# A third slot for group C's cached keys and values while the units of group B run, asked for three units ahead by two engines

## The reference, cut to what matters

```
A (6 heads): dilated window attention over cache_a_k, cache_a_v        1024 positions
B (6 heads): attention over the 256 keys that an indexer picks          pages of cache_b_k, cache_b_v
C (4 heads): difference of two softmax maps                             pages of cache_c_k, cache_c_v
rows = pool[l, page_table]     # 8 pages of 128 positions per sequence
o = concat(A, B, C) @ w_o
```

## Time and profile before

| what | us |
|---|---|
| median of 3 runs | 1462.43 |
| the 3 runs | 1462.43, 1468.67, 1453.17 |
| the profiled execution, its own time | 1457.15 |
| its span, first to last instruction | 1455.0 |
| TensorE busy in it | 1352.8 (93%) |
| the units of layer one and two, about | 210 to 412, 920 to 1115 |

### The profile page before, as it was taken

The page is one execution under the profiler, slowest core; times in us unless marked ns, Lnnn a source line. Parts: engine busy times, 40 slices in busy tenths (PEclk is TensorE's granted clock), DMA queues, the critical chain, the costliest instruction groups (busy, mean ns, idle before and its releaser), DMA issues.

```text
span 1455.0 us, 23578 instructions
## 1 busy us (share of the span) xinstructions
PE 1352.8 (93%) x8214; PEld 856.8 (59%) x8214; DVE 504.0 (35%) x1315; ACT 286.0 (20%) x711; POOL 62.4 (4%) x271
## 2 busy tenths in 40 slices
PE   6989899988799999999999999998889999999998
PEld 1544346655566666666665543665556567767775
DVE  1102677864254110011012057777534611100112
ACT  0011123333223101100003111433332220100001
POOL 1100000001001000000001000000000100000000
PEclk9999999999899999999999999999999999999999
DMA  7788979999943567887764577899996537686563
GB/s 268 206 288 267 282 234 356 351 283 320 319 142 134 218 218 257 301 317 258 284 224 153 183 233 244 297 373 295 310 320 216 195 130 253 205 284 209 205 235 130
DMA packets 189567, 363.82 MB, mean 250 GB/s; under 512 B 22912, under 2 KB 140360, under 8 KB 187786
## 3 DMA queue, kind: packets, MB, share of 16 engines
q1 hardware_dynamic: 165200, 350.19, 70.6%
q10 hardware_dynamic: 24250, 12.14, 3.3%
HBM read 354.17 MB, written 58.40 MB: 284 GB/s over the span
## 4 chain that ended last, share of the span: by engine, by line
PE 47%; issue 36%; DVE 6%; DMA 3%; SPq 2%; DVEq 2%; ACT 2%; ACTq 1%; POOLq 0%; POOL 0%
PE psf L1004 14%; PE psf L1422 9%; PE psf L1337 4%; PE psf L1192 3%; DMA ring<-in_tiles 3%; PE psf L1026 2%; PE psf L1235 2%; DVE m L1582 2%; DVEq L1585 1%; PE psf L1077 1%; PE psf L1405 1%; SPq L486 1%; PE psf L1281 1%; PE psf L1334 1%; PE psf L1265 1%
## 5 line engine op out<-in xcount | busy, mean ns | idle before, releaser
L1004 PE MATMUL psf<-hT,ring 128*128 128x320 f32 x1440 | 399.2, 435 | 9.6 <-DMA ring<-in_tiles 7.7
L1004 PEld LDWEIGHTS psf<-hT,ring 128*128 128x128 f32 x1440 | 270.5, 190 | 137.9 <-issue 18.2
L1422 PE MATMUL psf<-big,ring 128*128 128x320 f32 x1024 | 280.2, 435 | 4.3 <-DMA ring<-in_tiles 2.2
L1422 PEld LDWEIGHTS psf<-big,ring 128*128 128x128 f32 x1024 | 194.6, 191 | 90.5 <-issue 6.2
L1798 DVE TENSOR_TENSOR big<-sq 128x320 f32<-128x320 f32 x64 | 31.5, 492 | 258.1 <-ACT sq L973 257.8
L1508 DVE TENSOR_SCALAR rstd<-psf,adaT 128x256 f32<-128x256 f32 x32 | 15.4, 482 | 252.9 <-PE psf L1422 237.6
L1582 DVE MAX8 m<-workbuf 64x8 f32<-64x1032 f32 x64 | 78.5, 1226 | 3.0
L931 ACT ACTIVATE sq<-xT 128x320 f32<-128x320 f32 x32 | 15.0, 470 | 324.3 <-DVE xT L1512 324.3
L1584 DVE MATCH_REPLACE8 workbuf<-m,workbuf 64x1032 f32<-64x1032 f32 x64 | 77.4, 1209 | 0.0
L1192 PE MATMUL psf<-big,qs 128*32 128x512 f32 x512 | 70.6, 640 | 6.9 <-issue 5.6
L1026 PE MATMUL psf<-ring,cz 128*32 128x512 f32 x384 | 63.6, 673 | 14.4 <-DVE cz L1456 8.4
(11 more groups left out here) (182 smaller groups left out, 1215.9 us busy)
## 6 DMA issues: line engine op xcount, KB each, us to landing
ring<-in_tiles SPq DMA_DIRECT2D x284, 512.0 KB, 4.4
big<-in_cache_a SPq DMA_DIRECT2D x64, 768.0 KB, 7.1
out_cache_a<-in_cache_a SPq DMA_DIRECT2D x64, 768.0 KB, 5.9
big<-in_pool_bk SPq DMA_DIRECT2D x128, 192.0 KB, 3.7
big<-in_pool_bv SPq DMA_DIRECT2D x128, 192.0 KB, 4.6
big<-in_pool_cv SPq DMA_DIRECT2D x256, 64.0 KB, 4.2
big<-in_pool_ck SPq DMA_DIRECT2D x128, 64.0 KB, 4.1
big<-in_pool_ck ACTq DMA_DIRECT2D x128, 64.0 KB, 4.5
```

What stands on the lines that cost most here:

```text
L1004: ins = pe.matmul(ps[:, 0:T], ring[:, s, k, :], rhs[:, k, :], start=k == 0, stop=k == KD - 1)
L1422: ins = pe.matmul(bank[6 + m % 2][:, 0:T], ring[:, s, k, :], uT[:, KD * q + k, :], start=q + k == 0, stop=q == 3 and k == KD - 1)
```

## The change

In the units of B, C's blocks get three slots instead of two. The third lies in `hT`: its first 1024 columns for keys, the next 1024 for values. A unit of B takes slot `(n - 8) % 3` (`c_slot`), a unit of A its `u.s` as before; `c_loaded` counts what each slot has received. The number of bytes loaded is the same.

- Units 0 to 9: C's values are still asked for two units ahead by SyncE, all eight pages, but now ahead of the values of A or B.
- Units 10 to 15: C's values are asked for three units ahead, behind the wait for `u_o` of the unit that used the slot. SyncE issues pages 0 to 3, after the eight pages of B's values; ScalarE issues pages 4 to 7, after C's keys.
- For units 10 to 15 ScalarE waits for `u_o` of unit n before it issues C's keys of unit n+3 (a slot of three is free only then).

```diff
--- before.py
+++ after.py
@@ -219,8 +219,10 @@
         big = sb("big", [P, 2 * SLOT])
         kv = big[:, :].rearrange("p (s w) -> p s w", s=2)
         k_in, v_in = ([kv[:, s, at:at + A_W].rearrange("p (j w) -> p j w", j=NPG) for s in range(2)] for at in (K_AT, V_AT_))
-        ck_in, cv_in = ([kv[:, s, at:at + NPG * P].rearrange("p (j w) -> p j w", j=NPG) for s in range(2)]
-                        for at in (CK_AT, CV_AT))
+        free = hT[:, :, :].rearrange("p k t -> p (k t)")
+        ck_in, cv_in = ([x.rearrange("p (j w) -> p j w", j=NPG)
+                         for x in (*(kv[:, s, at:at + NPG * P] for s in range(2)), free[:, NPG * P * n:NPG * P * n + NPG * P])]
+                        for n, at in enumerate((CK_AT, CV_AT)))
         uT = big[:, 0:FF // P * T].rearrange("p (m t) -> p m t", t=T)
         adarow = sb("adarow", [P, 512])
         PTi = adarow
@@ -308,8 +310,8 @@
         ld_ik = [sem(f"ld_ik{b}") for b in range(NB)]
         ld_k = [sem(f"ld_k{s}") for s in range(2)]
         ld_v = [sem(f"ld_v{s}") for s in range(2)]
-        ld_ck = [sem(f"ld_ck{s}") for s in range(2)]
-        ld_cv = [sem(f"ld_cv{s}") for s in range(2)]
+        ld_ck = [sem(f"ld_ck{s}") for s in range(3)]
+        ld_cv = [sem(f"ld_cv{s}") for s in range(3)]
         ld_dist = sem("ld_dist")
 
         st_dist = sem("st_dist")
@@ -455,6 +457,23 @@
             i = u.n // 2
             return (128 + 4 * PAGES) * l + (128 + PAGES * (i - 3) if u.second else 32 * (i + 1))
 
+        def c_slot(u):
+            return (u.n - NB) % 3 if u.second else u.s
+        def c_loaded(l, u):
+            a_layer, till = (sum(c_slot(v) == c_slot(u) for v in UNIT[:n]) for n in (UNITS, u.n + 1))
+            return PAGES * (a_layer * l + till)
+        def c_pages(eng, l, u, at, half, pages):
+            s = c_slot(u)
+            for j in pages:
+                eng.dma_start((ck_in, cv_in)[half][s][:, j, :],
+                              a["pool_cv" if half else "pool_ck"][ds(at[j] + l * N_PHYS, 1), :, P * u.second:P * u.second + P]
+                              .rearrange("o p w -> (o p) w")).then_inc((ld_ck, ld_cv)[half][s], 16)
         @block.sync
         def _(sp):
             def load(t):
@@ -499,10 +518,6 @@
 
             def load_b(l, u, at, half):
                 load_pages(l, at, a["pool_bv" if half else "pool_bk"], 0, (k_in, v_in)[half][u.s], (ld_k, ld_v)[half][u.s])
-            def load_c(l, u, at, half):
-                load_pages(l, at, a["pool_cv" if half else "pool_ck"], P * u.second, (ck_in, cv_in)[half][u.s],
-                           (ld_ck, ld_cv)[half][u.s])
 
             row = REP * NDIST
 
@@ -565,7 +580,7 @@
                         load_a(l, UNIT[0], 1, d - 4)
                     if d in (6, 7):
                         at = pages(0, CHECKED) if d == 6 else at
-                        load_c(l, UNIT[0], at, d - 6)
+                        c_pages(sp, l, UNIT[0], at, d - 6, range(NPG))
                     if d in (9, 10):
                         if d == 9:
 
@@ -575,7 +590,7 @@
                         load_a(l, UNIT[1], 1, d - 11)
                     if d in (13, 14):
                         at = pages(1, CHECKED) if d == 13 else at
-                        load_c(l, UNIT[1], at, d - 13)
+                        c_pages(sp, l, UNIT[1], at, d - 13, range(NPG))
                     d += 1
                 for t in MID[l][:RING - 1]:
                     load(t)
@@ -586,7 +601,7 @@
                         load_b(l, u, at, 0)
                     else:
                         load_a(l, u, 0, 0, 1)
-                        load_c(l, u, at, 0)
+                        c_pages(sp, l, u, at, 0, range(NPG))
 
                 at = pages(2, CHECKED)
                 sp.wait_ge(u_s.sem, u_s.done(l, 0))
@@ -603,11 +618,14 @@
                         load(MID[l][u.n + RING - 1])
 
                     sp.wait_ge(u_o.sem, u_o.done(l, u.n))
+                    if then.n < NB + 2:
+                        c_pages(sp, l, then, was, 1, range(NPG))
                     if then.second:
                         load_b(l, then, was, 1)
                     else:
                         load_a(l, then, 1, 0, 1)
-                    load_c(l, then, was, 1)
+                    if after and after.n >= NB + 2:
+                        c_pages(sp, l, after, at, 1, range(NPG // 2))
                     if u.n >= UNITS - 2 - RING:
                         load(MIXOUT[l][u.n - UNITS + 2 + RING])
 
@@ -863,13 +881,6 @@
                     n += 1
                 feature(LATE[0], late_bank(0))
 
-                def load_c_keys(u, at):
-                    for j in range(NPG):
-                        act.dma_start(ck_in[u.s][:, j, :],
-                                      a["pool_ck"][ds(at[j] + l * N_PHYS, 1), :, P:2 * P].rearrange("o p w -> (o p) w")
-                                      ).then_inc(ld_ck[u.s], 16)
                 def turned_unit(u):
 
                     act.wait_ge(u_tp.sem, u_tp.done(l, u.n))
@@ -913,7 +924,11 @@
                     if NB <= u.n + 3 < UNITS:
 
                         at = pages(UNIT[u.n + 3].b, CHECKED)
-                        load_c_keys(UNIT[u.n + 3], at)
+                        if u.n + 3 >= NB + 2:
+                            act.wait_ge(u_o.sem, u_o.done(l, u.n))
+                        c_pages(act, l, UNIT[u.n + 3], at, 0, range(NPG))
+                        if u.n + 3 >= NB + 2:
+                            c_pages(act, l, UNIT[u.n + 3], at, 1, range(NPG // 2, NPG))
                     for k in slots[1:]:
                         turned_item(k - 1)
                         exp_item(k)
@@ -1159,12 +1174,12 @@
                 def keys_wait(u):
 
                     pe.wait_ge(ld_k[u.s], loaded(l, u))
-                    pe.wait_ge(ld_ck[u.s], PAGES * (NB * l + u.n // 2 + 1))
+                    pe.wait_ge(ld_ck[c_slot(u)], c_loaded(l, u))
 
                 def values_wait(u):
 
                     pe.wait_ge(ld_v[u.s], loaded(l, u))
-                    pe.wait_ge(ld_cv[u.s], PAGES * (NB * l + u.n // 2 + 1))
+                    pe.wait_ge(ld_cv[c_slot(u)], c_loaded(l, u))
 
                 def logits(u):
 
@@ -1185,7 +1200,7 @@
                         for c in range(4):
                             if q < 2:
                                 rhs = (k_in[u.s][:, 4 * q:4 * q + 4, P * c:P * c + P] if c < 3
-                                       else ck_in[u.s][:, 4 * q:4 * q + 4, :])
+                                       else ck_in[c_slot(u)][:, 4 * q:4 * q + 4, :])
                             else:
                                 rhs = zT[:, u.k + c if c < 3 else u.kc, t0:t0 + NT]
                             masked = u.second and c < 3
@@ -1228,7 +1243,7 @@
                         for c in range(4):
                             if j < NPG:
                                 lhs = PT[:, j, G * c:G * c + G]
-                                rhs = v_in[u.s][:, j, P * c:P * c + P] if c < 3 else cv_in[u.s][:, j, :]
+                                rhs = v_in[u.s][:, j, P * c:P * c + P] if c < 3 else cv_in[c_slot(u)][:, j, :]
                             else:
                                 v0 = u.v + P * c if c < 3 else u.vc
                                 lhs, rhs = PT[0:TS, j, G * c:G * c + G], vs[0:TS, v0:v0 + P]
```

## The result

| | before | after |
|---|---|---|
| median, 20 runs each (us) | 1455.44 | 1468.14 |
| the profiled execution (us) | 1457.15 | 1469.61 |
| its span (us) | 1455.0 | 1467.5 |

The ratio after to before is 1.008, with a 95% interval of 1.0062 to 1.0098: the change makes the kernel 0.8% slower, some 12 us. The forecast was 0.6% faster. The time stands just above the top of the range given (1468.0), and it moved the other way. One of the 20 executions before took 3440.32 us; the ratio goes by fast executions alone and leaves it out.

A forecast was written before the change was run, and what follows sets the result against it. TensorE was taken as the bound, interrupted by loads late from SyncE's issuing. 1457.15 - 19.1 + 10 + 2 = 1450.1 us, plus 3 us towards the median, gave 1453 us, range 1440 to 1468.

The forecast's parts named there:

- What bounds the kernel now: Units of B: TensorE bounds, interrupted by late loads, because SyncE issues all the time in a 14.3 us round.
- all five waits: TensorE in B's units: four waits for C's values, 9.8 us, and one for B's keys, 1.3; expected to go, 11.1 us.
- ScalarE issues more, in a worse place: ScalarE, units 7 to 12: four more pages ahead of the next unit's copies cost 10 us, ends 3 and 27.
- The walk: Unit 10's ScalarE timeline: copies move to 353.6 us, 3.0 us late, idle takes in 1.4, the unit costs 1.6 us.
- The clock comes back: TensorE's matmuls behind the removed waits and from 380 to 400 us regain full clock: 8.0 us gained.
- new gaps and the clock: Late ScalarE lengthens TensorE's gap before L1220, which can drop the clock: one drop, 2 us, ends 0 and 12.
- forecast gain of 19.1 us: TensorE in B's units: 11.1 us of waits removed and 8.0 us of clock won back.
- The added wait: ScalarE's new wait for unit 10's values ahead of its pages: starts them 0.5 us later.
- The rest at nothing: C's values ahead of A's, TensorE's changed semaphores, the third slot in `hT` and unchanged bytes: costed at nothing.
- ScalarE becomes the bound: Rival: from `u_o` to the next copies, ScalarE takes 11.7 us a unit against TensorE's 10.3; 1469 us, median 1472, chance 0.10.
- The DMA engines are the bound: Rival: the 16 DMA engines are full, the wait moves to B's values; 1461 us, median 1464, chance 0.12.
- ScalarE's issuing is hidden: Rival: ScalarE's idle time while exponentials wait for VectorE takes in the four pages; 1439 us, median 1442, chance 0.12.

The follow-up runs named there:

- run 4: Changed kernel with C's keys and values of a page in one DMA, eight on ScalarE and sixteen on SyncE a unit: 0.9902 of the kernel before.
- run 11: Kernel before, two slots, no added wait; ScalarE issues pages 4 to 7 of C's values behind the previous unit's copies, units 9 to 14: ratio 0.9875.
- Run 10: Changed kernel with the first of ScalarE's three copies made by VectorE, in the units of B alone: 0.9931 of the kernel before.
- run 7: Kernel before with only ScalarE's wait for unit n's values added ahead of C's keys, units 10 to 15: ratio 1.0015.
- run 8: Changed kernel, but ScalarE issues C's keys ahead of the wait for `u_o` and only the values behind it: 1.0006 of the kernel before.
- Run 2: Kernel before, two slots and old SyncE order, with ScalarE issuing pages 4 to 7 of C's values behind C's keys and a `u_o` wait: ratio 1.008.
- run 3: Changed kernel with ScalarE's four pages of C's values issued behind the next unit's three copies instead of ahead: 0.9932 of the kernel before.

## Why the prediction was wrong

- *What bounds the kernel now*: right. SyncE's issuing made C's values late; with 20 issues instead of 24 its round took 12.0 us (12.2 forecast), and all five waits went. The nearness of the two rounds is in part luck: the 12.0 holds 10.9 us of issuing (no tile among it, which the 12.2 counted) and pauses.
- *ScalarE issues more, in a worse place*: this step failed. It was put at 10 us with ends of 3 and 27. The changed kernel stands 1.008 - 0.990 = 0.018, 26 us, above run 4, and 30 us above run 11; this difference holds the clock too. Two things in the step were wrong. First, the list of what waits behind the copies named the values and the later exponentials, but not the logits: their last part (q = 2) waits for `u_nset`, the first copy. The order of TensorE's work ahead of the prediction has the same hole: it lets `logits(n+1)` wait for the keys alone. In the trace of before no matmul waited for this copy, so I walked the delay past it. (The walk put the copies of unit 11 at 353.6 us, and they began at 353.64: luck, since unit 10 ended 0.9 us later than before and twelve pages took 6.56 us, not 7.6.) Run 10 shows that this copy carried nearly all. Second, the cover: I let six units take in the pages for nothing because their copies had not stood behind "issue". With twelve pages all twelve stood behind it.
- *The clock comes back*, and *new gaps and the clock*: these failed with it. The two terms together were a gain of 8.0 - 2 = 6 us. In the changed kernel the stage's matmuls are busy 6.8 us longer instead. The clock is at 1.00 from 380 to 400 us as forecast, but behind the new gaps it falls: behind the 1.64 us wait in unit 10 the values took 3.03 us, against 1.95. The place of the gaps was wrong too: L1220's wait did not grow, the new ones are in the logits. Where the waits are gone and ScalarE is not late, much of the forecast gain of 19.1 us is there: 0.0098 x 1455.7 = 14.3 us in run 4 and 0.0125 x 1459.2 = 18.2 in run 11. Run 11's interval holds 19.1, that of run 4 ends just short of it.
- *The added wait*: priced at 0.5 us from unit 10. In unit 12 of the kernel before the pages began 4.8 us before the values ended (365.79 and 370.55), so this was no price for all units. Alone the wait is indeed not measurable (run 7), but with late copies it costs 0.7%, 10 us (run 8), which fits a closed loop. A wait has to be priced in the schedule that the change makes, not in the one before.
- *The rest at nothing*: holds as far as was measured. Run 2, without third slot and new order, has the changed kernel's time.
- Of the rivals, *ScalarE becomes the bound* is what happened, at its place (from `u_o` to the copies) and with its loss (26 to 30 us, the clock in it, against the 27 + 4 forecast), but I gave it 0.10. Its time, 1469 us for the profiled execution, was 1469.61; so close a hit is luck, since the 1469 counts the 8.0 us of clock as won back, which they were not. *The DMA engines are the bound* fell: in 350 to 360 us they moved 349 GB/s where it was 307, and runs 3, 4 and 11 are faster with the same bytes. The Trainium skill ("DMA: Bandwidth & Descriptors", section "Issuing engines are not separate DMA queues") calls the time to issue usually small beside the DMA itself. For one page that is so here, half a microsecond beside a landing of 4.2 us; but 24 of them in a row were the bound of a 14.3 us round, and run 11, which moves four of them to another engine, is 1.25% faster. *ScalarE's issuing is hidden* comes true in part once the pages stand behind the copies: run 3 gains 10 us of the 18 that this rival had.
- The time against the range flatters the forecast: it was built on the median of three executions, 1462.43, and that of 20 is 7.0 us lower. The ratio, 1.008 against a forecast of 0.994, is the fair measure.

## What to carry to other kernels

When work is moved from one queue to another, list every instruction that waits for anything queued behind the new place, the smallest copy too, and look for a wait whose time is zero now: that is where a delay enters unseen. A DMA costs its issue time on the engine that issues it (here half a microsecond, for 64 KB as for 192 KB); put it where that engine would be idle, ahead of nothing that another engine waits for, or merge two into one. A wait added on a late engine for a result that depends on this engine closes a loop, so price both together. And when the sum of the waits does not explain the time, compare the busy time of the same instructions: here a larger part of the loss was TensorE's clock behind the gaps than the gaps themselves.

## What the runs showed of the hardware

- Issuing costs about the same for 64, 128 and 192 KB: eight DMAs took 4.62, 4.92 and 3.74 to 4.97 us in the rows above. The exceptions, 6.49 and 7.31 us for eight, are in run 4.
- Pages beyond the slack cost 0.8 to 0.9 us each where their issue takes 0.55. The rest may be the loop and TensorE at its lower level (a clock of 0.83 in stretches with the new gaps); how it divides in these runs was not measured.
- The DMA share can pass 1: it was 1.11 at 349 GB/s from 350 to 360 us in the changed kernel, where it had been 0.97 at 307. A share near 1 had not meant that the engines could move no more.
- The same matmuls of the stage took 167.2 us of busy time before, 174.0 after and 158.5 in run 10, at granted clocks of 0.92 and 0.95, 0.92 and 0.90, and 0.98 in both layers.
